# Expert products by jobs of up to 160 rows, with row lists built by indirect DMAs, in a decoder layer with a mixture of experts

## The reference

```
logits = x @ router_w + router_b                 # 520 x 32
top_v, top_i = top_k(logits, 4)
gates = softmax(top_v)
per chosen expert e:
    hh = x @ e_w_in[e] + e_b_in[e]               # 1024 -> 2048
    gate, up = split(hh); gate = min(gate, 7); up = clip(up, -7, 7)
    act = gate * sigmoid(1.702 * gate) * (up + 1)
    y += gates[e] * (act @ e_w_out[e] + e_b_out[e])
x = layer_norm(2**0.25 * x + y)
```

## Time and profile before

| | |
|---|---|
| time of three runs | 1525.91, 1529.34, 1531.61 us (median 1529.34) |
| the profiled execution | 1530.08 us, span 1528.2 us |
| mean granted TensorE clock | 0.917 |
| instructions in the profile | 36296 |
| loaded and stored over the span | 461.09 MB |

### The profile page before, as it was taken

The page is one execution under the profiler, slowest core; times in us unless marked ns, Lnnn a source line. Parts: engine busy times, 40 slices in busy tenths (PEclk is TensorE's granted clock), DMA queues, the critical chain, the costliest instruction groups (busy, mean ns, idle before and its releaser), DMA issues.

```text
span 1528.2 us, 36296 instructions
## 1 busy us (share of the span) xinstructions
PE 1303.2 (85%) x12462; PEld 569.4 (37%) x12463; DVE 542.3 (35%) x1812; ACT 151.3 (10%) x330; POOL 298.3 (20%) x246
## 2 busy tenths in 40 slices
PE   5998888997579998999999999989799797897970
PEld 5885333573123332333333333333233232332320
DVE  1994521237423332333333333333233232232325
ACT  0003232021000000000000000000000000000002
POOL 7000131100112221222222222222122121121213
PEclk9999679876789998999999999999899998898985
DMA  9600432116699999997899999999979979869493
GB/s 306 194 3 32 154 109 110 42 57 248 255 365 410 381 410 415 390 404 297 320 414 395 412 413 399 413 408 415 416 287 414 416 292 418 340 231 419 178 374 113
DMA packets 93350, 461.09 MB, mean 302 GB/s; under 512 B 12848, under 2 KB 37133, under 8 KB 43549
## 3 DMA queue, kind: packets, MB, share of 16 engines
q1 hardware_dynamic: 74315, 432.95, 69.9%
q0 software_dynamic: 16640, 20.04, 5.9%
q10 hardware_dynamic: 2370, 7.78, 1.3%
HBM read 446.70 MB, written 19.29 MB: 305 GB/s over the span
## 4 chain that ended last, share of the span: by engine, by line
PE 55%; DMA 12%; issue 5%; DVE 1%; SPq 0%; POOLq 0%; POOL 0%; ACT 0%; ACTq 0%; DVEq 0%
PE pu L1517 33%; PE py L1529 19%; DMA ring<-in_e_in 11%; PE pu L1510 2%; PE raw L1500 1%; DMA xq<-x_rows,idx 0%; DVE bn L1724 0%; DMA ring<-acc_rows 0%; DVE ring L1740 0%; DVE mv L1734 0%; SPq L220 0%; POOLq L1316 0%; POOL ring L1492 0%; POOLq L1474 0%; DVE mv L1726 0%
## 5 line engine op out<-in xcount | busy, mean ns | idle before, releaser
L1517 PE MATMUL pu<-ring,xgT 128*32 128x512 f32 x5248 | 611.7, 613 | 49.6 <-DMA ring<-in_e_in 49.6
L1517 PEld LDWEIGHTS pu<-ring,xgT 128*32 128x32 f32 x5248 | 164.8, 111 | 435.5 <-issue 333.2
L1529 PE MATMUL py<-ring,hid 128*32 128x256 f32 x5248 | 310.2, 390 | 3.8 <-issue 3.8
L1455 POOL DMA_INDIRECT acc_rows<-y,idx x82 | 129.2, 1575 | 841.1 <-ACT y L1598 831.2
L1695 DVE TENSOR_SCALAR gg<-pu 128x256 f32<-128x256 f32 x82 | 34.8, 425 | 495.4 <-PE pu L1517 495.4
L1529 PEld LDWEIGHTS py<-ring,hid 128*32 128x32 f32 x5248 | 165.6, 112 | 110.7 <-issue 14.5
L1709 DVE STREAM_TRANSPOSE hid<-hq 128x256 f32<-128x256 f32 x82 | 36.5, 445 | 234.2 <-ACT y L1598 234.2
L722 PE MATMUL pair<-xt,ring 128*128 128x260 f32 x448 | 100.2, 386 | 15.8 <-DMA xt<-in_xT 15.8
L1592 ACT ACTIVATE ss<-gg 128x256 f32<-128x256 f32 x82 | 34.2, 417 | 748.2 <-DVE gg L1695 748.2
L1448 POOL DMA_INDIRECT xq<-x_rows,idx x85 | 88.8, 1044 | 48.0 <-issue 32.0
L722 PEld LDWEIGHTS pair<-xt,ring 128*128 128x128 f32 x448 | 85.9, 192 | 28.8 <-DMA xt<-in_xT 15.4
(11 more groups left out here) (246 smaller groups left out, 751.7 us busy)
## 6 DMA issues: line engine op xcount, KB each, us to landing
ring<-in_e_in SPq DMA_DIRECT2D x256, 1024.0 KB, 14.9
ring<-in_e_out SPq DMA_DIRECT2D x128, 1024.0 KB, 16.8
ring<-in_w_in SPq DMA_DIRECT2D x3, 1536.0 KB, 13.1
ring<-in_w_o SPq DMA_DIRECT2D x1, 4096.0 KB, 13.2
ring<-in_w_in SPq DMA_DIRECT2D x6, 512.0 KB, 13.3
xt<-in_xT SPq DMA_DIRECT2D x2, 1040.0 KB, 9.8
xtok<-in_x_prompt POOLq DMA_DIRECT2D x4, 512.0 KB, 3.7
x_rows<-conv ACTq DMA_DIRECT2D x4, 512.0 KB, 9.0
```

Source lines behind the costliest of these rows:

```text
L1455: nc.gpsimd.indirect_dma_start(out=acc_quarters, out_offset=bass.IndirectOffsetOnAxis(ap=idx8[:, c:c + 1], axis=0), in_=y[:, i], in_offset ...
L1517: mm = nc.tensor.matmul(pu[quarter(c)], xgT[:, k], w[:, :, c * QC:(c + 1) * QC], start=False, stop=k == KT - 1, skip_group_check=True)
L1529: mm = nc.tensor.matmul(py[quarter(c), 0:QC], hid[:, 2 * q + f], w[:, f, c * QC:(c + 1) * QC], start=q == 0 and f == 0, stop=q == FT // 2 ...
```

## The change

An expert's rows are now one job of up to 5 groups, 160 rows (an expert with more would have several jobs). For each unit of weights TensorE runs the calls of all groups of the job and then lets the unit go (`up`, `down`). The order is up(s+1), down(s). The code is written out for three steps of the loop and in each for five sizes of a job; `for_groups` picks the size by a tree of branches.

The search for slots and its product are gone. In `first_block` TensorE ranks each tile of 128 rows right after its routing (`rank`), VectorE works out a place in a list for each pair (`place_in_lists`), and GpSimd writes row number and gate there with an indirect DMA, four per tile and 20 in all (`list_rows`), into DRAM that was filled with empty entries. SP then loads the lists to SBUF, and `name_rows` reads a job's row numbers and gates from them. All buffers of the loop hold five groups: `xq` and `y` once (two and four single groups before), `pu` in five banks of PSUM. VectorE and ScalarE work on five groups whatever the job's size, with the results of ScalarE in five instructions, and GpSimd issues five gathers and five scatters per job. SP loads the units in the order in which they are used: up(s+1), then down(s). `ORDER` is another one: by groups the experts come as 2, 1, 3, 3, 3, 3, 2, 5, 2, 2, 2, 3, 2, 4, 2, 3, 2, 5, 1, 2, 4, 2, 3, 2, 3, 2, 5, 1, 3, 1, 3, 1. The table of jobs replaces that of groups (`job_table`, `job_rows`).

```diff
-MAXG = TOPK * R // GS + NE - 1
-NGT = MAXG + 8
-NWORD = MAXG // 3
+JG = 5
+JR = JG * GS
 MAXR = -(-R // GS)
+MAXN = -(-R // JR)
+MAXQ = JG * MAXN
+MAXJ = NE + (TOPK * R - NE) // JR
+NJT = MAXJ + 4
+NWORD = -(-MAXJ // 3) + 1
+AHEAD = 4
...
+            sp.wait_ge(copied, 48)
+            sp.wait_ge(listed, 16 * TOPK * (NT + 1))
+            for c in range(NQ):
+                sp.dma_start(lists[c * GS:(c + 1) * GS], lists_dram).then_inc(lists_in, 16)
...
+            def list_rows(i):
+                gp.wait_ge(placed_in_lists, i + 1)
+                if i == 0:
+                    gp.wait_ge(copied, 48)
+                for k in range(TOPK):
+                    nc.gpsimd.indirect_dma_start(
+                        out=lists_dram.rearrange("s q c -> (s q) c"),
+                        out_offset=bass.IndirectOffsetOnAxis(ap=spots[0:rows(i), i, k:k + 1], axis=0),
+                        in_=pairs[0:rows(i), i, k], in_offset=None,
+                        bounds_check=GS * NE * MAXQ - 1, oob_is_err=False).then_inc(listed, 16)
...
+            def rank(i):
+                pe.wait_ge(m_ready, i + 1)
+                pe.wait_ge(top_neg, i + 1 if i < NT - 1 else NT + 1)
+                pe.wait_ge(bf_ready, 2)
+                for j in range(i + 1):
+                    mm = nc.tensor.matmul(bS[0][:, (i + 1) * NE:(i + 2) * NE], trib[0:rows(j), 0 if j == i else 1],
+                                          memb[0:rows(j), j], start=j == 0, stop=j == i)
+                mm.then_inc(rank_done, 1)
...
+            def place_in_lists(lo, hi):
+                n, first = hi - lo, (lo + 1) % 2
+                two = slice(first, first + n)
+                d.wait_ge(rank_done, hi)
+                ranks = bS[0][:, (lo + 1) * NE:(hi + 1) * NE].rearrange("p (u e) -> p u e", e=NE)
+                if hi > NT:
+                    d.wait_ge(counted, 1)
+                for i in range(lo, hi):
+                    V.tensor_tensor(ranked[:, i - lo], oh2[:, first + i - lo],
+                                    ranks[:, i - lo].unsqueeze(1).broadcast_to([P, TOPK, NE]), ALU.mult
+                                    ).then_inc(ranks_read, 1)
+                d.wait_ge(ranks_read, hi)
+                ch.do(V.tensor_reduce(rank4[:, 0:n], ranked[:, 0:n], AX.X, ALU.add))
+                flat4 = lambda t: t.rearrange("p u k -> p (u k)")
+                ch.do(V.tensor_tensor(past[:, 0:n * TOPK],
+                                      C("step").unsqueeze(1).broadcast_to([P, n * TOPK, MAXR - 1]),
+                                      flat4(rank4[:, 0:n]).unsqueeze(2).broadcast_to([P, n * TOPK, MAXR - 1]), ALU.is_le))
+                ch.mark(V.scalar_tensor_tensor(flat4(spot[:, 0:n]), flat4(rank4[:, 0:n]), float(GS),
+                                               flat4(chosen4[:, lo:hi]), ALU.mult, ALU.add))
+                ch.do(V.tensor_reduce(flat4(wraps[:, 0:n]), past[:, 0:n * TOPK], AX.X, ALU.add))
+                ch.do(V.tensor_scalar(flat4(wraps[:, 0:n]), flat4(wraps[:, 0:n]), 1.0 - GS * NE * MAXQ, None, ALU.mult))
+                V.scalar_tensor_tensor(flat4(spots[:, lo:hi]), flat4(spot[:, 0:n]), float(MAXQ), flat4(wraps[:, 0:n]),
+                                       ALU.mult, ALU.add).then_inc(placed_in_lists, n)
...
-        xq = sb("xq", [P, 2, QC])
-        xgT = sb("xgT", [P, KT, GS])
-        hid = sb("hid", [P, FT, GS])
-        y = sb("y", [P, 4, QC])
-        gg = sb("gg", [P, QC])
-        uu = sb("uu", [P, QC])
-        ss = sb("ss", [P, QC])
-        hq = sb("hq", [P, QC])
-        onehot = sb("onehot", [P, NT + 1, NQ, GS], BF16)
-        pay = sb("pay", [P, NT + 1, 6], BF16)
-        gparts = sb("gparts", [P, NT + 1, NE, 3], BF16)
-        grest = sb("grest", [P, NT + 1, NE])
+        xq = sb("xq", [P, JG, QC])
+        xgT = sb("xgT", [P, JG, KT, GS])
+        hid = sb("hid", [P, JG, FT, GS])
+        y = sb("y", [P, JG, QC])
+        gg = sb("gg", [P, JG, QC])
+        uu = sb("uu", [P, JG, QC])
+        ss = sb("ss", [P, JG, QC])
...
+            last = job_count(sp)
+            with sp.Fori(1, MAXJ // 3 + 1) as t:
                 for i in range(3):
-                    before, last_but_one = end_of(3 * three + i + 1), end_of(3 * three + i)
-                    e = expert_at(3 * three + i + 2)
-                    for j in range(UNITS):
-                        load(e, (i + 2) % 3, j, last_but_one if j < ahead else before)
+                    s = 3 * t + i
+                    with sp.If(s + 1 < last):
+                        e = expert_of(s + 1)
+                        for k in range(KT):
+                            if k < 2:
+                                sp.wait_ge(up_done, KT * s - 1 + k)
+                            elif k < 6:
+                                sp.wait_ge(down_done, FT // 2 * s - 9 + k)
+                            else:
+                                sp.wait_ge(up_done, KT * s - 5 + k)
+                            load(e, k, up_at(3 + i, k))
+                    with sp.Else():
+                        sp.nop()
+                    with sp.If(s < last):
+                        e = expert_of(s)
+                        for q in range(FT // 2):
+                            sp.wait_ge(up_done, KT * s + 3 + q)
+                            load(e, KT + q, down_at(3 + i, q))
...
+            def gather(c):
+                for j in range(JG):
+                    nc.gpsimd.indirect_dma_start(
+                        out=xq[:, j], out_offset=None, in_=x1_quarters,
+                        in_offset=bass.IndirectOffsetOnAxis(ap=idx4[:, c, j:j + 1], axis=0),
+                        bounds_check=NQ * R - 1, oob_is_err=False).then_inc(gathered, 16)
+            def scatter(c):
+                for j in range(JG):
+                    nc.gpsimd.indirect_dma_start(
+                        out=acc_quarters, out_offset=bass.IndirectOffsetOnAxis(ap=idx4[:, c, j:j + 1], axis=0),
+                        in_=y[:, j], in_offset=None, compute_op=ALU.add,
+                        bounds_check=NQ * R - 1, oob_is_err=False).then_inc(scattered, 16)
...
+                    u = AHEAD * t + i
+                    with gp.If(u < last):
+                        gp.wait_ge(named, u + 3)
+                        gp.wait_ge(turned, u + 2)
                         gp.sem_inc(gathers, 1)
+                        gather((i + 2) % AHEAD)
+                        gp.wait_ge(scattered, 16 * JG * u)
                         gp.sem_inc(y_free, 1)
+                        gp.wait_ge(y_done, u + 2)
+                        gp.sem_inc(gathers, 1)
+                        scatter(i % AHEAD)
                     with gp.Else():
                         gp.nop()
+            gp.wait_ge(gathered, 16 * JG * (last + 2))
+            gp.wait_ge(scattered, 16 * JG * last)
...
+            def up(groups, step, rounds):
+                for j in range(groups):
+                    for c in range(NQ):
+                        nc.tensor.matmul(pu[quarter(c), j], chosen[:, :], brow[:, c],
+                                         start=True, stop=False, skip_group_check=True)
                 for k in range(KT):
+                    slot, nth = place(up_at(step, k))
+                    pe.wait_ge(unit_in[slot], 16 * nth + rounds)
                     w = unit(slot).rearrange("p (a n) -> p a n", a=2)
+                    for j in range(groups):
+                        for c in range(NQ):
+                            mm = nc.tensor.matmul(pu[quarter(c), j], xgT[:, j, k], w[:, :, c * QC:(c + 1) * QC],
+                                                  start=False, stop=k == KT - 1, skip_group_check=True)
+                    mm.then_inc(up_done, 1)
+            def down(groups, step, rounds):
+                for q in range(FT // 2):
+                    slot, nth = place(down_at(step, q))
+                    pe.wait_ge(unit_in[slot], 16 * nth + rounds)
+                    w = unit(slot).rearrange("p (f n) -> p f n", f=2)
+                    for j in range(groups):
+                        for f in range(2):
+                            for c in range(NQ):
+                                mm = nc.tensor.matmul(py[quarter(c), j], hid[:, j, 2 * q + f],
+                                                      w[:, f, c * QC:(c + 1) * QC],
+                                                      start=q == 0 and f == 0 and j % 2 == 0, stop=q == FT // 2 - 1 and f == 1,
+                                                      skip_group_check=True)
+                    mm.then_inc(down_done, 1)
+            def for_groups(groups, f, lo=1, hi=JG + 1):
+                if hi - lo == 1:
+                    f(lo)
+                    return
+                mid = (lo + hi) // 2
+                with pe.If(groups < mid):
+                    for_groups(groups, f, lo, mid)
+                with pe.Else():
+                    for_groups(groups, f, mid, hi)
...
+            last = job_count(pe)
+            with pe.Fori(0, -(-MAXJ // 3)) as t:
```

(45 more changed lines are left out.)

503 lines of the change are left out of this document (201 added, 302 removed).

## The result

The changed kernel takes 2218.2 us (median of four runs, 2209.2 to 2223.3), the kernel before 1528.5; the ratio is 1.451, its 95% interval 1.448 to 1.455. The forecast was 1803 with a range of 1455 to 1960, so the result lies 258 us above its upper end: the direction and the kind of cause were right, the size was short by 415 us. A 12-slot version with one copy of the products, found on the way, takes 1498.9 us, 0.981 of the kernel before (0.978 to 0.983).

A forecast was written before the change was run, and what follows sets the result against it. Before: TensorE and the weight stream in turn; after: TensorE, through code misses. Front 407, products with control 942, misses 331, clock 77 and tail 45 made 1802 us of span, forecast 1803, range 1455 to 1960.

The forecast's parts named there:

- Front: Work before the expert loop: its first product moves from 399.2 to 407 us, bounds 399 and 420.
- Products, clock: TensorE's products in the loop: 894 us at the same rate, plus 77 us of clock loss after stalls.
- Code: TensorE's jumps to absent code in the loop: 88 misses at 5 us, 440 us, of which 331 remain unhidden.
- the control: Value loads and branch trees on TensorE in the loop: 1.5 us a job, 48 us.
- cover: During up, TensorE's sequencer can be 3.4 us ahead when it jumps to down; 109 us hidden over 32 jobs.
- What decides whether a landing misses: TensorE's instruction store: 8 blocks, refilled in sequence; each jump over more than a block counts as a miss.
- Tail: From the last down product to the end: 45 us instead of 36.9, for four more result copies and scatters.
- the code costs little: Rival: TensorE's code is fetched ahead or kept, so the weight stream bounds, 1456 to 1485 us; chance 0.31 for 1456 to 1510.
- The row chain: Rival: gathers and scatters with one buffer each of `xq` and `y` set the step, 36 us, 1604 us; chance 0.04.
- The reuse: Rival: weights still pause with 18 slots, under 25 us in all, 1480 us at most alone; no separate chance.
- The signs: Loop trace if right: block fetches in the hundreds, 3 to 7 us issue gaps, clock under 0.95, GB/s under 330.

The follow-up runs named there:

- e5: As e2, with 12 weight slots instead of 18 and one step of code in TensorE's loop instead of three: 1497.1 us.
- e13: As e1, with the tree of tests replaced by five stretches in a row, each behind its own test of one size: 2548.8 us.
- e4: The kernel before, with 448 product calls that are never executed between up and down: 1538.0 us.
- e6: The kernel before, with two one-block stretches of never executed code, each behind its own test, between up and down: 1544.7 us.
- e7: The kernel before, with eight one-block stretches of never executed code, each behind its own test, between up and down: 5252.8 us.
- e11: The kernel before, with three one-block stretches of never executed code, each behind its own test, between up and down: 3711.7 us.
- e12: The kernel before, with five one-block stretches of never executed code, each behind its own test, between up and down: 4359.9 us.
- e1: The changed kernel with TensorE's loop over three-job steps ending after 11 rounds instead of 15: 2092.0 us.
- e2: As e1, with one copy of up and down per step, groups behind nested tests, instead of five copies: 1642.9 us.
- e8: As e1, with each load from the fourth job on bringing only 256 of a unit's 2048 columns: 1875.9 us.
- e10: As e1, five copies kept, with 12 slots and one step in the loop: 2184.2 us.
- e3: The kernel before, with 192 product calls that are never executed between up and down: 1541.1 us.

## Why the prediction was right in direction and 405 us short

Step by step, in its own terms and against the profiled span of 2207.4.

*Front:* 407 against 404.7. Right.

*Products, clock:* 894 + 77 = 971 busy against 1011.1, 40 us short. Most of it is the base: 6.99 and 3.59 us were one group each at a granted clock of 1.00, while 82 of them took 611.7 and 310.2 us, 922 without the bias, against the 894 of the forecast with it. In e5, with 21 us of "issue" and a clock of 0.96, the 10824 records take 926.0, which is 32 more than 894. The clock, 0.80 over the loop, then cost 85 us (1011.1 - 926.0) against the 77 forecast.

*Code:* the step that failed, "Counting a jump over more than a block as a miss [...]: 88 misses". With the control it had 48 + 331 = 379 us of idle time; the trace has 626.8, 248 more. The price of 5 us was right for a single landing among weights: where one stands alone, before the bias of jobs 7, 13, 19, 22 and 28, the gaps of the changed kernel are 4.6 to 5.9 us. The count was not. The five copies hang in a tree of tests, and a test inside a skipped half stands far away itself: size 5 is reached over three landings, not one, and leaving over an outer half is another. The trace shows it: before the down products of the three five-group jobs TensorE idles 19.2 to 22.5 us, before those of the ten three-group jobs 7.1 to 12.2. By the layout I estimate 65 landings for up, 67 for down and 10 returns, 142; 142 x 5 - 31 x 3.4 of cover = 605 us, against 622 of "issue". That more landings for the same bodies cost more is shown by e13. The 142 is not seen in the trace: two landings can share a block, and the same way of counting gave e13 only half of the idle time that it added. So that the count was short is shown, by how much against the price is open.

*What decides whether a landing misses:* I took the distance jumped, over a store of eight blocks that slides along the code. e4 refutes that, and e6, e7, e11 and e12 put in its place: the last eight blocks, wherever they are. The forecast came out of a wrong picture of the store and was right in direction only because each job of the changed kernel lands in more than eight (310 blocks for 32 jobs, 9.7 each); so much of it is luck. The page "Runtime: NRT & Kernel Launch" of the Trainium skill (Instruction fetch mechanics), cited there, gives TensorE's store 128 KiB in 16 KiB blocks as a FIFO, and e6 and e11 agree, eight against nine; its remark that a jump out of the current two pages stalls is not borne out by e4, whose 82 jumps over seven blocks fetched one block after 440 us. It also says that kernels prefer full unrolling where possible; here the unrolled copies cost 449 us (e1 against e2).

*Tail:* 45 against 164.8. 45.9 of these (2042.6 to 2088.5, GpSimd's last addition) are the tail as predicted; the other 119 are the idle rounds of TensorE, a second step that failed: the prediction put them at nothing without a word. Their working was at hand: a loop bounded for 45 jobs, 32 jobs, and a price for each jump.

Sum of the errors: -2 + 40 + 248 + 120 = 406, and 2207.4 - 1802 = 405.

*The rivals:* that the code costs little is refuted by e2 and e5. Its figure (1456 to 1485) is near what the change gives once the code stays on the core, 1497 in e5. The row chain doesn't bind in the changed kernel: VectorE waited 16 us in all before its 33 transposes of gathered rows. It begins to show in e5. The reuse holds: not one wait for weights in the loop.

*The signs:* hundreds of blocks, yes (383). A clock under 0.95, yes. Under 330 GB/s, yes (249). Gaps of 3 to 7 us: only where there is one landing; most are 7 to 23, and that alone would have told that several stand in a row. More in three-group jobs than in two-group ones, yes: 10.1 against 4.4 us on average before the down products.

## What to carry to other kernels

Count the blocks of code that one turn of a loop lands in, with the ends and one block ahead: in these runs eight stayed on TensorE, and the ninth cost every one of them in every turn. Copies of a body for each size were the dear way to handle a size known only at run time; one copy with small skips inside each unit did the same work 449 us faster, and choosing the buffer count so that one step of code serves all steps gave another 146. And an unexecuted round of a loop bounded for the worst case is not free: here 12 absent jobs, with 4 returns to the top, cost some 119 us at the very end of the span.

## What the runs showed of the hardware

- One landing in an absent block costs 5.1 to 5.6 us among the weights (e1) and 3.2 with an eighth of their traffic (e8); with the engines idle, blocks came 3.2 us apart (e11), and a skip that brings two took about 5 (the idle rounds). Extra landings among weights cost 2.7 to 2.8 us for each further block (e10, e13). For code that is mostly run straight through it is 1.0 us of "issue" a block, returns to the top included (e2 against e5: 200.1 against 21.0 us for 180 more blocks).
- Between eight and nine blocks a turn lies a factor of 2.4 in the whole kernel's time (1544.7 to 3711.7), by 256 records that are never executed.
- Seven blocks of dead code inside a hot loop cost 12 us over 82 turns (e4), no more than three blocks did (15 us, e3), single runs both.
- Fetches suffer from the kernel's own traffic: with an eighth of the weights' bytes they stalled TensorE a third less (e8).
